# Hybrid diffusion step on one core: output DMAs moved from ScalarE to SyncE, two weight splits moved later, and one mask of the decays' rest moved from ScalarE to GpSimd

## The chip, the cores and the metric

The kernel runs on 1 core of one Trainium2 chip. The metric is the device time in microseconds of one execution. Three runs of the kernel before gave 833.46, 833.5 and 834.12 us, median 833.5.

## The reference, cut to what matters

Two trunk layers, each the same: a modulated RMSNorm, one input projection whose columns go to three head groups, one output projection, then a mixture of experts. The third head group is a Mamba-2 scan in chunks of 128 tokens, done in two directions. Its decays are what one part of the change touches:

```python
da = (dt * a)                        # per token, head and direction
cs = jnp.cumsum(da, axis=-1)
seg = cs[..., :, None] - cs[..., None, :]
lmat = jnp.exp(jnp.where(lower, seg, -jnp.inf))
scores = jnp.einsum('bclhn,bcshn->bhcls', cm, bm) * lmat
y_diag = jnp.einsum('bhcls,bcshp->bclhp', scores, xd)
chunk_states = jnp.einsum('bclhn,bhcl,bclhp->bchpn', bm, decay_to_end, xd)
...
o = jnp.concatenate([o_a, o_b, o_c], axis=-1)
return o @ w_out, new                # new: a_k, a_v, b_k, b_v, h_f, h_b of the context tokens
```

There are 384 tokens in 3 tiles of 128: tile 0 holds the context tokens, tiles 1 and 2 the latent ones. The six members of `new` are outputs of the kernel (keys and values of tile 0, and the two final states of tile 0).

## The kernel before, in words

Each engine has its own program. All of them walk the same list of steps, `layer_steps(l)`, and do of each step what concerns them. The order of that list is therefore the order on every engine. Engines meet in semaphores.

*Weights.* Weights come from memory as fp32 in pieces of 1 MB (128x2048) into `ring`, a ring of 8 slots of which the attention part uses 5. SyncE (SP) issues these loads one after the other, in the order of the list `pieces`; before each it waits until the former piece in that slot is released. A piece of `w_ada` is released by the TensorE (PE) matmuls that use it (L620), a piece of `w_out` by the subtraction of its split. `pieces` follows the step list, so moving a step `("wsplit", 0)` moves the load of that piece of `w_out` and shifts which slots later pieces take.

*Splits.* The big products take a weight as the sum of two parts: ScalarE (ACT) copies the piece to a rounded type (`w_hi`, L1225 for the input projection, L1216 for the output projection) and VectorE (DVE) subtracts this from the original (L1644 and L1639). A step `("w_split", p)` does this for piece p of the input projection, a step `("wsplit", n)` for unit n of the output projection. Piece 4 is first needed by `("rows", 4, 0)`, unit 0 of the output projection by `("wout",)` at the end of the attention.

*The stage around the scan.* `("rows", p, m)` is half a product of the input projection for token tile m (L854, 12 matmuls). ACT then copies the finished rows of tile m out of PSUM (L1385 and L1387). Between these products stand, for each tile m:
- `("ssm_in", m)`: PE transposes (L891, L895, L901). GpSimd (POOL) writes `ud[:, 0]`, the triangular mask times the rounded decays, for both directions (L2118, two instructions of 128x1024). POOL waits for the former tile's `seg`, and after the masks it makes `yx` and `xdd` (L2130, L2135). ACT copies `xs` (L1415) and writes `cbw` in 8 instructions (L1425). DVE makes `skip` (L1863) and multiplies `cbw` (L1871).
- `("seg", m)`: PE sums the masks (L924). It waits for POOL's half of `ud` (`sig["ud"]`) and for ACT's half (`sig["ud_lo"]`). ACT takes the exponential (L1433), then writes the half for the next tile, `masked_rest(m + 1)` (L1231): the mask times the decays' rest, in 16 instructions of 128x128, 8 for each direction. DVE multiplies to `mm` (L1881).
- `("ssm_y", m)`: PE products (L938, L948 or L954). DVE adds `yx` to them (L1888), and for tiles 1 and 2 makes `hin` (L1897, L1904). For tile 0, ACT copies the state to `stout` (L1441) and issues two output DMAs (L1445).
- `("prep", m)`: normalisation and rotation of the rows on DVE (L1830 to L1840, L1668 to L1676), with two small ACT instructions. For tile 0, ACT then waits for DVE's end of it and issues four output DMAs (L1398).

*PSUM banks.* Seven banks are given out in turn, in PE's order. Four of these hand-overs matter: the second half of `seg` of tile 1 takes the bank of the rows of tile 1 (freed by L1387). The rows of tile 2, second group, take the bank of `ssm_y` of tile 0 (freed by L1888). The first `rows` with p = 4 take the bank of the transposed queries (freed by L1406). The second half of `seg` of tile 2 and the rows of tile 1, third group, take banks that DVE frees in L1888 and L1904 of tile 1.

*The attention.* `head_steps()` gives 12 pairs of heads: `scores` v (PE L987, L993, L1001; DVE maximum L1928; ACT exponential L1465), `scale` v (DVE L1949 to L1955), `turn` v (PE L1011, ACT L1481), `values` (PE L1026, DVE L1963), and `gate` (DVE L1981). Pieces of `w_ada` (PE L620) are strewn between. The step `("wsplit", 0)` stands ahead of `("scores", 4)`. `ada_turn` (PE L633) needs ACT's copy of the `ada` bank (L1202).

*Order on the queues.* ACT does its two sets of output DMAs in order among its other work. SP has nothing to issue between the last load for the rows and the first `w_ada` piece behind them.

Of the kernel before, what the change touches and what calls it, by code (L numbers as in the profile page):

```python
# [25 lines left out]
P = 128  # L26
# [6 lines left out]
SH, SG, DS = 8, 2, 512  # L33
# [168 lines left out]
def layer_steps(l):  # L202


    ada = [("ada", l, t, k) for t in (1, 2) for k in range(KD)]
    ahead = [("ada", l + 1, 0, k) for k in range(KD)] if l + 1 < DEPTH else []
    early = 3 if l else 0
    s = [("norm", 0)] + ada[:early] + [("w_split", 0), ("h_split", 0), ("w_split", 1), ("h_split", 1), ("w_split", 2), ("xbc",)]
    s += [("rows", p, m) for p in (0, 1) for m in range(TILES)]

    def rows(g, m):
        return [("rows", 2 * g, m), ("rows", 2 * g + 1, m)]
    s += [("rest",), ("ssm_in", 0)] + rows(1, 0) + [("seg", 0), ("prep", 0), ("w_split", 4)] + rows(1, 1)
    s += [("ssm_y", 0), ("ssm_in", 1), ("seg", 1), ("prep", 1)] + rows(1, 2) + [("w_split", 5), ("turn_qk", 0)]
    s += [("ssm_y", 1), ("ssm_in", 2), ("rows", 4, 0), ("seg", 2), ("rows", 4, 1), ("rows", 4, 2), ("turn_qk", 1), ("prep", 2)]
    s += [("rows", 5, m) for m in range(TILES)] + [("ssm_y", 2), ("silu_z",)]
    burst = early + 3
    s += ada[early:burst]
    heads = head_steps()
    at = heads.index(("scores", 2))  # L220
    heads[at:at] = [("ssm_off", 1)]
    at = heads.index(("scores", 3))
    heads[at:at] = [("ssm_off", 2)]
    at = heads.index(("scores", 4))
    heads[at:at] = [("wsplit", 0)]
    at = heads.index(("scores", 2))
    heads[at:at] = [("turn_qk", 2)]
    rest = ada[burst:8] + [("ada_turn", l, 1)] + ada[8:14]
    done = 0
    for i, h in enumerate(heads):  # L230
        s.append(h)
        want = min(len(rest), len(rest) * (i + 1) * 3 // (len(heads) * 2)) if i < len(heads) // 3 else \
            len(rest) // 2 + (len(rest) - len(rest) // 2) * (i + 1 - len(heads) // 3) // (len(heads) - len(heads) // 3)
        s += rest[done:want]
        done = want
    s += [("turn_mix",)] + ada[14:] + [("ada_turn", l, 2), ("wsplit", 1), ("wout",), ("norm", 1)] + ahead[:3]
    s += [("router",), ("hrow", 0), ("rank",), ("hrow", 1), ("hrow", 2), ("h_lo",)] + ahead[3:] + [("flag",)]
    if ahead:
        s.append(("ada_turn", l + 1, 0))
    return s + [("combine",)] + moe_steps(0) + [("more",)]  # L240


def build(nc, a, a_out):
# [73 lines left out]
    with ExitStack() as ctx:  # L317
# [805 lines left out]
        @block.sync  # L1123
        def _(sp):
            sp.dma_start(pcol, a["pcol"]).then_inc(pcol_in, 16)
            for half in range(2):
                sp.dma_start(xT[:, 4 * half:4 * half + 4, :], a["xT"][:, 4 * half:4 * half + 4, :]).then_inc(x_in[half], 16)

            def load(key):
                dst = slot(key)  # L1130
                kind, l, at = key[0], key[1], key[2:]
                if kind == "first":
                    src = a["first"][at[0]]
                elif kind == "ada":
                    t, k = at
                    src = a["w_ada"][l, k * P:(k + 1) * P, t * PIECE:(t + 1) * PIECE]
                elif kind == "xbc":
                    src, dst = a["w_xbc"][l, at[0]], dst[:, 0:2 * (XBC + DT)]
                elif kind == "win":
                    src = a["w_rows"][l, at[0]]  # L1140
                elif kind == "wout":
                    src = a["w_out"][l, OUT_UNITS[at[0]][0], OUT_UNITS[at[0]][1]]
                elif kind == "down":
                    src = a["w_down"][l, at[1]].rearrange("(f p) n -> p f n", p=P)
                    dst = dst.rearrange("p (f n) -> p f n", f=2)
                else:
                    src = a["w_gu"][l, at[1], 0 if kind == "gua" else 1]
                sp.dma_start(dst, src).then_inc(landed(key)[0], 16)

            until_experts = pieces[0:pieces.index(("gua", 0, 0, 0))]  # L1150
            for n, key in enumerate(pieces):
                if n == 3:
                    sp.dma_start(const, a["const"]).then_inc(const_in, 16)
                if n == RING + KD // 2:
                    sp.dma_start(par, a["par"]).then_inc(par_in, 16)
                former = former_in[key]
                if made_here(key):
                    continue
                if former:
                    sp.wait_ge(*release[former])  # L1160
                if place[key] < HELD and key not in until_experts:
                    sp.wait_ge(*done["down", 0, 0, NE - 1])
                load(key)
                l = key[1]
                if key != ("down", l, 0, NE - 1):
                    continue

                sp.wait_ge(sig["flag"], l + 1)
                over = sp.value_load(flag[0:1, l:l + 1], min_val=0, max_val=1)
                with sp.If(over != 0):  # L1170
                    for former in pieces[n - (RING - HELD) + 1:n + 1]:
                        sp.wait_ge(*release[former])
                    for i, extra in enumerate(more_pieces):
                        extra = (extra[0], l, *extra[1:])
                        if i >= RING - HELD:
                            former = more_pieces[i - (RING - HELD)]
                            sp.wait_ge(*release[(former[0], l, *former[1:])])
                        load(extra)
                    sp.wait_ge(*done["down", l, PASSES - 1, NE - 1])
            for c in range(0, KD, 2):  # L1180
                sp.wait_ge(*modulated(DEPTH, 0, c + 1))
                sp.dma_start(a_out[0][:, c:c + 2, :], hT[:, c:c + 2, :]).then_inc(y_out, 16)
            sp.wait_ge(y_out, 16 * KD // 2)
            for s in out_sem:
                sp.wait_ge(s, 16 * DEPTH)
# [3 lines left out]
        def _(act):  # L1189
# [36 lines left out]

            def masked_rest(m):

                for d, tri in enumerate(("incl_f", "incl_b")):
                    for h in range(SH):  # L1230
                        ins = act.activation(ud[:, 1, d, h, :], c_(tri), ACT.Copy,  # L1231
                                             scale=da_lo[:, m, SH * d + h:SH * d + h + 1])
                ins.then_inc(sig["ud_lo"], 1)
# [91 lines left out]
            for l in range(DEPTH):  # L1325
                for step in STEPS[l]:
# [61 lines left out]
                    elif kind == "prep":  # L1388
# [2 lines left out]
                        act.activation(nrm[:, 8:14], nrm[:, 0:6], ACT.Ln, bias=eps_col, scale=1.0 / HD).then_inc(act_step, 1)  # L1391
                        act.wait_ge(act_step, act_steps())
                        act.activation(nrm[:, 16:22], nrm[:, 8:14], ACT.Exp, scale=-0.5).then_inc(sig["brs"], 1)
                        if m == 0:

                            act.wait_ge(sig["prep"], per["prep"] * l + 1)
                            for i, c0 in enumerate((256, 384, OFF_B + 256, OFF_B + 384)):
                                act.dma_start(a_out[1 + i][0, l].rearrange("s k d -> s (k d)"), row[:, 0, c0:c0 + P])\  # L1398
                                    .then_inc(out_sem[i], 16)
                    elif kind == "turn_qk":  # L1400
                        m = arg[0]
                        for t in range(2):
# [33 lines left out]
                    elif kind == "ssm_y":  # L1436
                        if arg[0] == 0:
                            key = ("state", l, 0)
                            act.wait_ge(*full(key))
                            src = bank(key)  # L1440
                            ins = act.copy(stout.rearrange("p a b n -> p (a b n)"), src)  # L1441
                            ins.then_inc(*was_read(key))
                            act.wait_ge(*taken(key))
                            for d in range(2):
                                act.dma_start(a_out[5 + d][0, l].rearrange("(r h) p n -> (h p) r n", h=2),  # L1445
                                              stout[:, d, :, :]).then_inc(out_sem[4 + d], 16)
                    elif kind == "silu_z":

                        for m in range(TILES):
# [654 lines left out]
        def _(pool):  # L2104
# [4 lines left out]
            for l in range(DEPTH):  # L2109
                for step in STEPS[l]:  # L2110
# [6 lines left out]
                    for d, tri in enumerate(("incl_f", "incl_b")):  # L2117
                        ins = tt(ud[:, 0, d, :, :], c_(tri).unsqueeze(1).to_broadcast((P, SH, P)),  # L2118
                                 da_hi[:, m, 8 * d:8 * d + 8].bitcast(F32).unsqueeze(2).to_broadcast((P, SH, P)), ALU.mult)
                    ins.then_inc(sig["ud"], 1)  # L2120
                    if m == 0:
                        pool.wait_ge(*taken(("cum", l)))
# [52 lines left out]
```

## Time and profile before

| | us |
|---|---|
| median of 3 runs | 833.5 |
| the profiled execution | 832.95 |
| its span in the profile | 831.2 |
| PE busy / share of the span | 764.6 / 92% |
| PE weight loads | 574.4 / 69% |
| DVE | 586.2 / 71% |
| ACT | 477.7 / 57% |
| POOL | 46.2 / 6% |
| mean granted TensorE clock | 0.975 |

1.75 us of the profiled execution lie around the span. A busy share is a mean over the whole span. The stage of the change lies at about 84 to 146 us and its attention at 146 to 203 us in the first layer; in the second layer the same steps lie 396.7 us later up to the first `seg` and about 395 us later after it. The experts' part follows, up to 412 and 808 us.

### The profile page before, as it was taken

How to read it: one execution, taken by the hardware profiler on the slowest of the kernel's cores; microseconds unless marked ns; L12 is line 12 of the kernel's file. 1: busy time of each engine (PE TensorE's matmuls, PEld its weight loads, DVE VectorE, ACT ScalarE, POOL GpSimd, SP SyncE). 2: the span in 40 equal slices, each digit the busy share in tenths (PEclk: the TensorE clock that was granted, in tenths of full speed). 3: DMA queues.
4: the chain of work that ended last, by engine and by line, in shares of the span. 5: the costliest groups of instructions: out<-in, count | busy, mean ns of one | idle time of the engine just before them, and what ended most of it. 6: DMA issues, size and time to landing. Idle time of an engine off the chain costs nothing.

```text
span 831.2 us, 10722 instructions
## 1 busy us (share of the span) xinstructions
PE 764.6 (92%) x3980; PEld 574.4 (69%) x3980; DVE 586.2 (71%) x934; ACT 477.7 (57%) x768; POOL 46.2 (6%) x36
## 2 busy tenths in 40 slices
PE   4997989789999999999989998988998799999995
PEld 2565868356956888888766786844694688888874
DVE  4139676776359889999663866678544888999975
ACT  3043983465336777777543387456533687777752
POOL 0000631000000000000000063100000000000000
PEclk9999999979999999999999999989998999999998
DMA  9942032976437799999760213377540079999912
GB/s 366 423 172 100 3 126 58 415 285 255 153 151 278 262 377 358 373 374 359 266 277 19 61 42 110 119 304 255 209 146 0 22 251 377 365 366 377 355 63 79
DMA packets 33488, 185.98 MB, mean 224 GB/s; under 512 B 5136, under 2 KB 6288, under 8 KB 16400
## 3 DMA queue, kind: packets, MB, share of 16 engines
q1 hardware_dynamic: 30160, 184.11, 58.5%
q10 hardware_dynamic: 3264, 1.05, 0.5%
q8 instruction: 36, 0.59, 0.3%
q14 instruction: 28, 0.23, 0.1%
HBM read 182.53 MB, written 2.62 MB: 223 GB/s over the span
## 4 chain that ended last, share of the span: by engine, by line
PE 64%; DVE 7%; ACT 6%; issue 2%; ACTq 0%; DVEq 0%
PE psum L739 21%; PE psum L768 11%; PE psum L1056 8%; PE psum L854 4%; PE psum L825 4%; PE psum L791 3%; PE psum L620 2%; ACT ud L1231 2%; PE psum L1026 2%; PE psum L1070 1%; DVE h_lo L2064 1%; PE psum L1011 1%; PE psum L987 1%; PE psum L717 1%; PE psum L752 1%
## 5 line engine op out<-in xcount | busy, mean ns | idle before, releaser
L1724 DVE TENSOR_TENSOR split<-ring,split 128x2048 fp32r<-128x2048 f32 x96 | 219.9, 2291 | 27.7 <-ACT split L1306 25.1
L1306 ACT CAST split<-ring 128x2048 fp32r<-128x2048 f32 x96 | 183.6, 1912 | 18.2 <-PE psum L768 14.5
L739 PE MATMUL psum<-split,y_hi 128*128 128x512 f32 x512 | 162.8, 399 | 0.0
L739 PEld LDWEIGHTS psum<-split,y_hi 128*128 128x128 f32 x512 | 93.7, 188 | 19.6
L739 PE MATMUL psum<-split,y_lo 128*128 128x512 f32 x256 | 100.6, 393 | 0.0
L854 PE MATMUL psum<-ring_r,hT_hi 128*128 128x512 f32 x216 | 75.2, 403 | 6.2 <-ACT qkT L1406 3.6
L768 PE MATMUL psum<-split,hidT 128*128 128x512 f32 x256 | 70.3, 396 | 1.8 <-DVE hidT_lo L1729 1.8
L825 PE MATMUL psum<-hT,ring 128*128 128x384 f32 x192 | 69.2, 499 | 0.0
L768 PEld LDWEIGHTS psum<-split,hidT 128*128 128x128 f32 x256 | 47.4, 187 | 14.5 <-DVE hidT_lo L1729 3.7
L739 PEld LDWEIGHTS psum<-split,y_lo 128*128 128x128 f32 x256 | 48.0, 188 | 11.1
L854 PEld LDWEIGHTS psum<-ring_r,hT_hi 128*128 128x128 f32 x216 | 41.0, 193 | 16.6 <-issue 4.4
L2118 POOL TENSOR_TENSOR ud<-const,da_hi 128x1024 fp32r<-128x1024 f32 x12 | 27.2, 2288 | 437.8 <-DVE da_lo L1821 437.4
L825 PEld LDWEIGHTS psum<-hT,ring 128*128 128x128 f32 x192 | 34.2, 190 | 20.2 <-issue 2.5
L1246 ACT ACTIVATE row<-xT 128x384 f32<-128x384 f32 x40 | 20.4, 524 | 48.1 <-DVE xT L1656 44.8
L620 PE MATMUL psum<-ring,silu_c 128*32 128x512 f32 x320 | 41.2, 620 | 3.7 <-DMA ring<-in_w_ada 3.2
L1465 ACT ACTIVATE hT<-psum,att 128x384 f32<-128x384 f32 (+1 forms) x48 | 24.0, 506 | 35.6 <-DVE att L1936 19.0
L1656 DVE SCALAR_TENSOR_TENSOR xT<-psum,mods,xT 128x128 f32<-128x128 f32 x64 | 23.6, 413 | 25.0 <-PE psum L1056 20.5
L768 PE MATMUL psum<-split,hidT_lo 128*128 128x512 f32 x128 | 39.8, 392 | 0.0
L854 PE MATMUL psum<-w_hi,hT_hi 128*128 128x512 f32 x72 | 29.6, 412 | 4.3 <-DVE dtw L1775 4.3
L1056 PE MATMUL psum<-m_hi,split 128*128 128x384 f32 x128 | 33.4, 337 | 0.0
L1056 PE MATMUL psum<-o_hi,split 128*128 128x384 f32 x128 | 33.2, 336 | 0.0
L1639 DVE TENSOR_TENSOR split<-ring,split 128x2048 fp32r<-128x2048 f32 x8 | 18.3, 2292 | 17.7 <-ACT split L1216 17.7
(258 smaller groups left out, 1340.4 us busy)
## 6 DMA issues: line engine op xcount, KB each, us to landing
ring<-in_w_gu SPq DMA_DIRECT2D x64, 1024.0 KB, 5.0
ring<-in_w_ada SPq DMA_DIRECT2D x40, 1024.0 KB, 6.3
ring<-in_w_down SPq DMA_DIRECT2D x32, 1024.0 KB, 5.3
ring<-in_w_rows SPq DMA_DIRECT2D x12, 1024.0 KB, 4.9
ring<-in_first SPq DMA_DIRECT2D x8, 1024.0 KB, 14.7
ring<-in_w_out SPq DMA_DIRECT2D x8, 1024.0 KB, 5.0
ring<-in_w_xbc SPq DMA_DIRECT2D x8, 784.0 KB, 8.5
par<-in_par SPq DMA_DIRECT2D x1, 1632.0 KB, 12.1
```

The source lines that it names most:

```text
L620: last = pe.matmul(psum[32 * q:32 * q + 32, 7, :], silu_c[:, k, :], w[:, q * 512:(q + 1) * 512], start=(k == 0), stop=(k == KD - 1), skip_ ...
L739: last = pe.matmul(dst, x[:, g, t, :], w[:, j, :], start=(t == 0 and i == 0), stop=(t == KD - 1 and i == 2))
L768: last = pe.matmul(psum[:, b, :], x, w[:, half * 512:(half + 1) * 512], start=(e % EPG == 0 and i == 0), stop=(e % EPG == EPG - 1 and i == ...
L791: last = pe.matmul(dst[:, 0:TOK], src[:, g, c * P:(c + 1) * P], selT[:, g, :], start=(i == 0 and g == 0), stop=(i == 1 and g == NG - 1))
L825: last = pe.matmul(bank(("xbc", l, c))[:, 0:TOK], w[:, kk, c * P:(c + 1) * P], hT[:, k, :], start=(k == 0), stop=(k == KD - 1))
L854: last = pe.matmul(dst, x[:, k, tok], w[:, j, :], start=(k == 0 and i == 0), stop=(k == KD - 1 and i == 2))
L1056: last = pe.matmul(dst[:, 0:TOK], w[:, k, cols], x[:, k, :], start=(part == 1 and k == 0 and i == 0), stop=(part == 0 and k == 3 and i == 2))
L1306: act.copy(splits[n % SPLITS][:, 0, :], slot(key)).then_inc(raised("whi", l, p), 1)
L1465: act.activation(probs[:, u % 8, 0:w], src[:, 0:w], ACT.Exp, bias=att[:, 1, u:u + 1], scale=SCALE, accum_out=att[:, 2, u:u + 1]).then_inc( ...
L1656: ins = stt(xT[:, c, part], src[:, part], mods[:, l, gate + c, j:j + 1], xT[:, c, part], ALU.mult, ALU.add)
L1724: tt(lo, slot(unit_key(l, p, n)), hi.bitcast(F32), ALU.subtract).then_inc(raised("wlo", l, p), 1)
L2118: ins = tt(ud[:, 0, d, :, :], c_(tri).unsqueeze(1).to_broadcast((P, SH, P)), da_hi[:, m, 8 * d:8 * d + 8].bitcast(F32).unsqueeze(2).to_bro ...
```

## The change

- The four row outputs and the two state outputs of each layer are issued by SP, in a new function `store(l)`, just before the first `w_ada` load behind the pieces of the rows. ACT loses the wait for `prep` and six DMA issues in each layer.
- `("w_split", 4)` moves from behind `("prep", 0)` to behind `("ssm_in", 1)`, ahead of `("seg", 1)`.
- `("wsplit", 0)` moves from ahead of `("scores", 4)` to behind `("scale", 11)`, the last of the scales.
- `masked_rest(m)` for m = 1 and 2 does only the second direction on ACT (8 instructions in place of 16). POOL does the first direction in one instruction of 128x1024 more, behind its two of the same tile.

```diff
-    s += [("rest",), ("ssm_in", 0)] + rows(1, 0) + [("seg", 0), ("prep", 0), ("w_split", 4)] + rows(1, 1)
-    s += [("ssm_y", 0), ("ssm_in", 1), ("seg", 1), ("prep", 1)] + rows(1, 2) + [("w_split", 5), ("turn_qk", 0)]
+    s += [("rest",), ("ssm_in", 0)] + rows(1, 0) + [("seg", 0), ("prep", 0)] + rows(1, 1)
+    s += [("ssm_y", 0), ("ssm_in", 1), ("w_split", 4), ("seg", 1), ("prep", 1)] + rows(1, 2) + [("w_split", 5), ("turn_qk", 0)]
...
-    at = heads.index(("scores", 4))
+    at = heads.index(("scale", PAIRS - 1)) + 1
     heads[at:at] = [("wsplit", 0)]
...
+            def store(l):
+                sp.wait_ge(sig["prep"], per["prep"] * l + 1)
+                for i, c0 in enumerate((256, 384, OFF_B + 256, OFF_B + 384)):
+                    sp.dma_start(a_out[1 + i][0, l].rearrange("s k d -> s (k d)"), row[:, 0, c0:c0 + P]).then_inc(out_sem[i], 16)
+                sp.wait_ge(*taken(("state", l, 0)))
+                for d in range(2):
+                    sp.dma_start(a_out[5 + d][0, l].rearrange("(r h) p n -> (h p) r n", h=2), stout[:, d, :, :])\
+                        .then_inc(out_sem[4 + d], 16)
+            behind_rows = [pieces[pieces.index(("w_hi", l, 5)) + 1] for l in range(DEPTH)]
...
+                if key in behind_rows:
+                    store(key[1])
...
-                for d, tri in enumerate(("incl_f", "incl_b")):
+                for d, tri in ((0, "incl_f"), (1, "incl_b"))[1 if m else 0:]:
...
-                        if m == 0:
-                            act.wait_ge(sig["prep"], per["prep"] * l + 1)
-                            for i, c0 in enumerate((256, 384, OFF_B + 256, OFF_B + 384)):
-                                act.dma_start(...)
...
-                            act.wait_ge(*taken(key))
-                            for d in range(2):
-                                act.dma_start(...)
...
+                    if m:
+                        ins = tt(ud[:, 1, 0, :, :], c_("incl_f").unsqueeze(1).to_broadcast((P, SH, P)),
+                                 da_lo[:, m, 0:8].unsqueeze(2).to_broadcast((P, SH, P)), ALU.mult)
                     ins.then_inc(sig["ud"], 1)
```

## Rows read from the trace of the kernel before

**Rows 1.** Chain of waits, second layer: start us, us, engine, tile, line.
```profile
494.79 4.74 ACT ud L1231 x16
...
503.09 1.90 ACT ring_r L1225
...
507.61 3.20 ACT cbw L1425 x8
...
511.76 4.73 ACT ud L1231 x16
...
556.52 1.81 ACT split L1216
...
558.42 2.29 DVE split L1639
560.72 0.94 DVE att L1928 x2
```

**Rows 2.** Timeline, PE weight loads; in brackets idle time before and its releaser.
```profile
505.59 0.76 PEld L924 LDWEIGHTS psum<-ud,sides 128*128 128x128 f32 x4 [1.11 <-ACT row L1387]
508.04 0.19 PEld L854 LDWEIGHTS psum<-ring_r,hT_hi 128*128 128x128 f32 x1 [1.69 <-DVE ring_r L1644]
519.75 0.19 PEld L854 LDWEIGHTS psum<-ring_r,hT_hi 128*128 128x128 f32 x1 [1.95 <-issue]
524.76 0.19 PEld L854 LDWEIGHTS psum<-ring_r,hT_hi 128*128 128x128 f32 x1 [0.51 <-issue]
...
129.13 0.19 PEld L854 LDWEIGHTS psum<-ring_r,hT_hi 128*128 128x128 f32 x1
...
162.47 0.13 PEld L620 LDWEIGHTS psum<-ring,silu_c 128*32 128x32 f32 x4 [2.63 <-DMA ring<-in_w_ada]
...
168.44 0.18 PEld L633 LDWEIGHTS psum<-const,ada_rows 128*128 128x128 f32 x1 [4.78 <-ACT ada_rows L1202]
```

**Rows 3.** Timeline, POOL, second layer: the masks of tiles 1 and 2.
```profile
493.94 3.76 POOL L2118 TENSOR_TENSOR ud<-const,da_hi 128x1024 fp32r<-128x1024 f32 x2 [0.22 <-PE psum L924]
...
512.10 4.07 POOL L2118 TENSOR_TENSOR ud<-const,da_hi 128x1024 fp32r<-128x1024 f32 x2
```

**Rows 4.** Timeline, DVE: second layer's scan stage, then the first layer's attention.
```profile
495.92 2.19 DVE L1830 TENSOR_TENSOR tmp<-row 128x384 f32<-128x384 f32 x1
...
512.21 1.29 DVE L1881 TENSOR_TENSOR mm<-psum,cbw 128x512 f32<-128x512 f32 x2
...
524.22 0.42 DVE L1904 TENSOR_TENSOR hin<-psum,hin 128x256 f32<-128x256 f32 x1
...
159.99 0.48 DVE L1955 TENSOR_SCALAR hT<-hT,att 128x128 f32<-128x128 f32 x2
162.88 2.29 DVE L1639 TENSOR_TENSOR split<-ring,split 128x2048 fp32r<-128x2048 f32 x1 [2.40 <-ACT split L1216]
...
171.47 1.02 DVE L1928 TENSOR_REDUCE att<-psum 128x1 f32<-128x384 f32 x2 [1.68 <-PE psum L1001]
```

**Rows 5.** Timeline, ACT's queue, second layer: the output issues.
```profile
501.18 1.81 ACTq L1398 DMA_DIRECT2D out<-row  x4
...
506.06 0.95 ACTq L1445 DMA_DIRECT2D out<-stout  x2
```

**Rows 6.** Timeline, PE, first layer: the scores of pair 6.
```profile
172.88 1.22 PE L987 MATMUL psum<-qkT 64*128 64x256 f32 x4
```

**Rows 7.** Timeline, SP's queue, first layer: the load of output unit 0.
```profile
148.95 0.33 SPq L1148 DMA_DIRECT2D ring<-in_w_out  x1
```

**Rows 8.** Stretches: us, busy of PE, PEld, DVE, ACT, POOL; granted clock, DMA share, GB/s.
```profile
123.00:127.00 4.00, 3.90 (x10) 3.11 (x11) 3.97 (x6) 3.88 (x10) 0.00 (x0) 0.57 0.20 82
...
160.00:168.40 8.40, 1.45 (x11) 0.35 (x10) 5.89 (x11) 4.72 (x15) 0.00 (x0) 0.76 1.01 422
168.40:175.40 7.00, 6.93 (x36) 4.00 (x36) 4.10 (x13) 1.92 (x9) 0.00 (x0) 0.56 0.64 268
...
553.00:566.00 13.00, 10.10 (x54) 5.43 (x57) 10.14 (x26) 4.92 (x15) 0.00 (x0) 0.65 0.54 212
```

More of the change, by code:

```diff
@@ L1393, in _ @@
                         act.activation(nrm[:, 16:22], nrm[:, 8:14], ACT.Exp, scale=-0.5).then_inc(sig["brs"], 1)
-                        if m == 0:
-                            act.wait_ge(sig["prep"], per["prep"] * l + 1)
-                            for i, c0 in enumerate((256, 384, OFF_B + 256, OFF_B + 384)):
-                                act.dma_start(a_out[1 + i][0, l].rearrange("s k d -> s (k d)"), row[:, 0, c0:c0 + P])\
-                                    .then_inc(out_sem[i], 16)
                     elif kind == "turn_qk":
@@ L1440, in _ @@
                             src = bank(key)
-                            ins = act.copy(stout.rearrange("p a b n -> p (a b n)"), src)
-                            ins.then_inc(*was_read(key))
-                            act.wait_ge(*taken(key))
-                            for d in range(2):
-                                act.dma_start(a_out[5 + d][0, l].rearrange("(r h) p n -> (h p) r n", h=2),
-                                              stout[:, d, :, :]).then_inc(out_sem[4 + d], 16)
+                            act.copy(stout.rearrange("p a b n -> p (a b n)"), src).then_inc(*was_read(key))
                     elif kind == "silu_z":
```

## The prediction, written before the result was known

> **What bounds the kernel now.** I read the page's chain of waits first. In the experts' part it is PE from end to end, and nothing there is touched. In the second layer's scan stage and attention it leaves PE for ACT and DVE, and those are the steps that the change moves [rows 1]. The chain of the first layer is only followed from 167 us on, so there I read PE's idle time in the timeline. It shows the same stalls of PE 396.7 us earlier.
>
> In the scan stage PE stops four times in the second layer [rows 2]. At 505.59 it waits 1.11 us for the row copy that frees a bank. At 508.04 it waits 1.69 us for DVE, which stands in the split of piece 4. At 519.75 it waits 1.95 us for the copy of the transposed queries. At 524.76 it waits 0.51 us for the bank that DVE's L1904 frees, started at 524.22 [rows 4]. The first two are waits for ACT's issues and for split 4, which the chain holds at 503.09 [rows 1].
>
> In the attention of the first layer PE stands still for most of 160 to 168.4 us: 1.45 us busy in 8.4 [rows 8]. First it waits 2.63 us for a `w_ada` piece, then 4.78 us for ACT's `ada` copy [rows 2]. ACT is late because DVE's maximum of pair 4 is queued behind output split 0: DVE waits 2.40 us for ACT's half and then works 2.29 us [rows 4]. The second layer has the same in its chain: 1.81 us of ACT's half, 2.29 us of DVE's, then the maximum at 560.72 [rows 1].
>
> **Part 1: scan stage.** Second layer, by its own clock times.
>
> ACT loses half of the masks of tiles 1 and 2. Sixteen took 4.74 and 4.73 us [rows 1], so 2.37 us each time. It loses the issues, 1.81 + 0.95 us [rows 5], the wait for `prep` in front of them, and split 4 (1.90 us, [rows 1]) up to a later place. The issues cost SP the same 2.8 us, and there they are hidden: SP issues nothing until the rows of tile 2 are done, and both waits of `store` end before that. I put this part at 0.
>
> ACT would so reach `cbw` of tile 1 some 8 us sooner, but PE's product of tile 0 has to be ready first, and that stays where it is, at about 503. I let `cbw` start at 503.85 in place of 507.61 [rows 1], 3.8 us sooner. So the two stalls of 1.11 and 1.69 go, and PE does the rows of tile 2 from 505.3 in place of 508.04.
>
> What is late next is DVE. In front of its `mm` of tile 1, at 512.21 before [rows 4], now stands split 4: `cbw` done 507.0, ACT's half 1.90 to 508.9, DVE's half 2.29 more. Beside it POOL does three masks in place of two. One takes 3.76/2 = 1.88 us [rows 3]. DVE's L1830, issued at 495.92 beside POOL's pair, took 2.19 us and ended at 498.11, 0.41 us after the pair at 497.70 [rows 3, 4]. So a DVE instruction with two SBUF inputs waits for the end of the POOL instruction that runs. That makes up to 1.88 us for each POOL instruction met, and I count 0.75 for split 4: `mm` then starts at 508.9 + 0.75 + 2.25 = 511.9. PE arrives for it at 511.5 and waits 1.6 us for its end at 513.1, where it came at 514.2 before.
>
> The Trainium skill has this as a rule (SBUF — State Buffer, "Who interferes with whom"): the pair shared by DVE and GpSimd is an exclusive lock for a whole instruction. The trace agrees, by the 2.19 us.
>
> From `mm` to L1904 DVE is busy without a gap, 524.22 − 512.21 = 12.0 us [rows 4]. With the same sequence behind 511.9 and one more lock of 0.1 to 1.9 us (I take 0.1: the maximum of two instructions that wait already) L1904 comes at 524.0, 0.25 us sooner. PE's next products wait for it, so the stage gives **0.25 us in the second layer**, although ACT gave up 9 us. Bounds: 2.7 us sooner if nothing on DVE is late, and 3.5 us later if DVE's half of the split and one instruction behind it each meet one full POOL mask more.
>
> In the first layer the same point is at 129.13, not at 524.76 − 396.7 = 128.06 [rows 2]. PE was the later one there, since its clock was at its lower level (granted 0.57) from 123 to 127 [rows 8]. If DVE sets the time now in this layer too, PE gets there at 127.8: **1.3 us in the first layer**, low clock or not. Bounds: 3.5 later and 3.7 sooner, as above.
>
> **Part 2: attention, first layer.** DVE ends the scale of pair 2 at 160.47 [rows 4], in the new timing 1.3 sooner, at 159.1. With no split ahead of it the maximum of pair 4 starts there, in place of 162.88 + 2.2 = 165.1: 6.0 us sooner. ACT's exponential and `ada` copy follow, if the last piece of `w_ada` is there. The load of output unit 0 stood before it on SP [rows 7], at 422 GB/s [rows 8] 1.05 MB = 2.48 us of a saturated DMA. It goes to the back, so the piece lands 1.3 + 2.48 = 3.8 us sooner, at 158.7 in place of 162.47, just behind PE's scores 4. So the wait of 2.63 goes nearly whole, and `ada_turn` comes at 162.4 in place of 168.44 [rows 2]. In the new list `scores 5` stands ahead of it, so PE fills the gap of the copy.
>
> What comes last from here: DVE does the maximum 4, scale 3 and the gate until 162.8, and maximum 5 there in place of 171.47 [rows 4]: 8.7 us sooner. PE does `scores 6` at 164.0 in place of 172.88 [rows 6]: 8.9 us. Part of this is clock: from 168.4 to 175.4 PE ran at a granted 0.56 after its 8.4 us of idleness [rows 8], and I count about 1.6 us of that as saved, since the stops left are of 1.2 us at most. From there on PE is busy almost without a gap to the end, with all pieces landed ahead, so 8.9 us carry through.
>
> At the end split 0 stands behind the last scale. ACT's half (1.9) delays the copies of the last two `turn`s. PE's fifth block of `values` works from pairs 8 and 9 meanwhile and covers most of it. I take 1.0 us as left, of 0 to 1.9. DVE's half is before `turn_mix`, where DVE idles. Sum of the first layer: −8.9 + 1.0 = **−7.9 us**, the 1.3 of its stage included.
>
> **Attention, second layer.** DVE's maximum of pair 4 could start 4.6 us sooner, at 556.05 (scale 2 and `mods` end then) in place of 560.7 [rows 1]. But PE ran at a granted 0.65 over 553 to 566 [rows 8], and its `scores 5` ended at 560.5, so that the next maximum is only 3.6 us sooner. At `turn` 4 and `scores` 7 I still find 2.7 to 2.8. The clock may recover sooner, as PE loses its stops of 560 to 564: then up to 4.6. I take **−3.0**, with 0.25 of the stage in it. At the end PE comes to `values` 5 as the copies are done: 0.
>
> **Sum.** −7.9 − 3.0 = −10.9 on the profiled execution's own time, 832.95 (span 831.2 and 1.75 around it): 822.1. The median of the runs stands 0.55 above that execution, so the forecast is 822.6.
>
> **Rivals.**
>
> *A. Only one of the two stalls of the first layer is collected.* The DMA has a share of 1.01 over 160 to 168.4 [rows 8], so the queue may stay full and the piece come late, or the low clock return in the gap that is left. For it: both stalls lie behind each other. Against it: the load that goes away is as long as the wait. Then the first layer gives its stage's 1.3, the 2.48 of the load and 0.5 more, −4.3, and the second −2: 833.5 − 6.3 = 827.2.
>
> *B. The mask gives nothing or costs.* The Trainium skill warns (Perfetto Trace Analysis, "Optimizing Scalar/DVE Operations") that moving work between GpSimd and DVE may not help, because they share a port. That is this rival in general form. By rows: two further masks of 1.88 us in each layer [rows 3] held against DVE's chain of 12.0 us, −0.25 and −1.3 become +1.6 and +0.6, the rest unchanged: 822.6 + 3.8 = 826.4.
>
> *C. Slower: DVE loses the port in the scan stage.* Split 4 waits for one whole mask more before `mm`, and the first and the fifth instruction of `prep` 1 for one each: 3 × 1.88 = 5.6 us a layer [rows 3]. PE, which waits for `mm` and for L1904, then stands long enough for its clock to fall as it did at 123 us, where 4 us at 0.57 cost 4 × 0.43 = 1.7 us [rows 8]. The stages so give +7.3 in each layer in place of −0.25 and −1.3, beside the attention's −9.35: 833.5 + 14.6 − 9.35 = 838.8. It decides from 9.35 / 2 = 4.7 us a layer. For it: DVE's later instructions there mostly have two SBUF inputs, and the clock did fall in this stage. Against it: POOL's pair with one DVE instruction let in between took 4.07 in place of 3.76 us [rows 3], so the two take turns, and `mm` itself reads PSUM.
>
> *D. No change*, as PE's later work only waits elsewhere: the experts' part has PE in the chain throughout, and begins when the output projection ends, so I see no place.
>
> **How the numbers follow.** Forecast 0.55, A 0.17, B 0.17, C 0.07, D 0.04. The range reaches from 818.5 (the second layer gives 4.6, the stages 1 us each more, the tail nothing) up to A with a fall of the clock on top, 829.5. A measurement of this kernel tells 0.2% (1.7 us) from no change. Faster 0.55 + 0.17 + 0.17 = 0.89, same 0.04, slower 0.07.
>
> **What would show it.** ACT's `cbw` of tile 1 3 to 4 us sooner, but DVE's L1904 by under 1 us. The load of output unit 0 behind thirteen `w_ada` loads of the layer, and not behind seven. PE's stop before `ada_turn` in the first layer about 1.2 us in place of 4.78, and the granted clock near 1.0 behind it. Output projection from about 194.9 in place of 202.8. If L1904 comes over 2 us later than before in its layer, B or C is true; if PE still waits over 2 us for the `w_ada` piece, A is. The forecast is wrong if the interval from first `scores` to output projection shrinks by less than 5 us in the first layer.

## The result: 12 us faster, 821.4 us for a forecast of 822.6

The changed kernel takes 821.36 us (median of 4 runs, 819.86 to 825.34), the kernel before 833.48 beside it (4 runs, 832.57 to 834.12). The ratio is 0.9863, 95% interval 0.9826 to 0.9900. The profiled execution took 819.86, its span is 817.7 us in place of 831.2, and its mean granted clock (TensorE's clock as the hardware granted it, 1.00 being the upper of its two levels) 0.989 in place of 0.975.

The span is 13.5 us shorter. Read at fixed points of PE's program (milestones) in both traces, these are: 0.2 before the first layer's stage, 1.2 in its scan stage up to the product behind L1904, 0.1 from there to the scores of pair 0, 6.2 in its attention. Then 0.3 in the experts' part, 0.1 in the second layer's scan stage, 4.7 in its attention, and 0.6 behind it. So the two attentions give 11 of 13.5 us; the scan stages, from which ACT lost most work, 1.3.

PE's stops that answer to [rows 2], from the timeline of the weight loads (idle time before and its releaser in brackets). L1644, L1881, L1888, L1904 of before are L1646, L1883, L1890, L1906 here.

```profile
505.31 1.86 PEld L938 LDWEIGHTS psum<-xs,mm 128*128 128x128 f32 x16 [1.65 <-DVE mm L1883]
510.20 0.30 PEld L854 LDWEIGHTS psum<-ring_r,hT_hi 128*128 128x128 f32 x2 [1.38 <-issue]
515.27 0.77 PEld L924 LDWEIGHTS psum<-ud,sides 128*128 128x128 f32 x4 [1.56 <-DVE y L1890]
516.55 0.30 PEld L854 LDWEIGHTS psum<-ring_r,hT_hi 128*128 128x128 f32 x2 [0.52 <-issue]
...
127.69 0.30 PEld L854 LDWEIGHTS psum<-ring_r,hT_hi 128*128 128x128 f32 x2 [0.51 <-issue]
...
158.46 0.16 PEld L620 LDWEIGHTS psum<-ring,silu_c 128*32 128x32 f32 x8 [0.16 <-DMA ring<-in_w_ada]
162.18 0.42 PEld L633 LDWEIGHTS psum<-const,ada_rows 128*128 128x128 f32 x4 [1.39 <-ACT ada_rows L1215]
187.72 0.66 PEld L1026 LDWEIGHTS psum<-pT,row 128*64 128x64 f32 x8 [1.13 <-issue]
```

The stops of 1.11 and 1.69 us are gone and others stand there: 1.65 for DVE's `mm`, 1.56 for its L1890. In the attention the 2.63 us for the `w_ada` piece are 0.16, the 4.78 for ACT's copy 1.39. PE's scores of pair 6, at 172.88 before [rows 6]:

```profile
163.56 0.70 PE L987 MATMUL psum<-qkT 64*128 64x256 f32 x4
```

DVE in the second layer's scan stage, which answers to [rows 4]. DVE is busy without a gap from the half split at 500.74 to L1906 at 516.01:

```profile
498.94 1.28 DVE L1873 TENSOR_TENSOR cbw<-cbw,psum 128x512 f32<-128x512 f32 x2 [2.12 <-ACT cbw L1432]
500.74 3.30 DVE L1646 TENSOR_TENSOR ring_r<-ring,ring_r 128x2048 fp32r<-128x2048 f32 x1 [0.52 <-ACT ring_r L1238]
503.97 1.28 DVE L1883 TENSOR_TENSOR mm<-psum,cbw 128x512 f32<-128x512 f32 x2
505.17 1.05 DVE L1832 TENSOR_TENSOR tmp<-row 128x384 f32<-128x384 f32 x1
506.72 1.67 DVE L1670 TENSOR_TENSOR tmp<-row,const 128x384 f32<-128x384 f32 x1
...
516.01 0.42 DVE L1906 TENSOR_TENSOR hin<-psum,hin 128x256 f32<-128x256 f32 x1
```

POOL beside it [rows 3], with the new mask (L2123), and ACT's `cbw` with the split behind it [rows 1]:

```profile
485.83 3.76 POOL L2120 TENSOR_TENSOR ud<-const,da_hi 128x1024 fp32r<-128x1024 f32 x2 [0.23 <-PE psum L924]
489.54 2.21 POOL L2123 TENSOR_TENSOR ud<-const,da_lo 128x1024 fp32r<-128x1024 f32 x1
...
500.00 5.80 POOL L2120 TENSOR_TENSOR ud<-const,da_hi 128x1024 fp32r<-128x1024 f32 x2
505.76 2.21 POOL L2123 TENSOR_TENSOR ud<-const,da_lo 128x1024 fp32r<-128x1024 f32 x1
```

```profile
495.71 3.20 ACT cbw L1432 x8
498.91 1.81 ACT ring_r L1238
```

SP's queue, first layer: the stores, and the load of output unit 0 at its new place (148.95 before, [rows 7]).

```profile
103.94 1.78 SPq L1154 DMA_DIRECT2D out<-row  x4
106.50 0.94 SPq L1157 DMA_DIRECT2D out<-stout  x2
...
165.54 0.33 SPq L1148 DMA_DIRECT2D ring<-in_w_out  x1
```

The stretches of [rows 8] (us; busy of PE, PEld, DVE, ACT, POOL; granted clock; DMA share; GB/s). The clock stood at 0.57, 0.76 and 0.65 in them and is at its upper level (1.00) in all three. The second layer lies some 8 us earlier here; over the same steps of it, 544.8 to 557.8, the clock is 1.00 too.

```profile
123.00:127.00 4.00, 2.88 (x13) 2.02 (x13) 3.99 (x5) 2.75 (x7) 0.00 (x0) 1.00 0.00 0
160.00:168.40 8.40, 6.59 (x56) 4.27 (x56) 8.05 (x25) 5.59 (x21) 0.00 (x0) 1.00 1.01 420
553.00:566.00 13.00, 11.33 (x92) 6.30 (x92) 11.76 (x37) 11.16 (x40) 0.00 (x0) 1.00 0.50 173
```

This holds for this execution only. The same kernel was profiled once more later (e9 below); there the clock fell in both scan stages and in the second attention:

```profile
123.00:127.00 4.00, 4.00 (x14) 3.11 (x14) 3.97 (x7) 2.88 (x8) 0.00 (x0) 0.71 0.00 0
511.50:515.50 4.00, 4.00 (x13) 3.11 (x12) 3.95 (x6) 2.42 (x7) 0.00 (x0) 0.63 0.01 2
545.00:558.00 13.00, 11.19 (x72) 6.31 (x71) 11.09 (x34) 6.76 (x27) 0.00 (x0) 0.77 0.52 181
```

### The profile page after: what moved, and what is told of

Read it like the earlier page. It is cut to its first block, busy times and chain, and to the rows that moved or that the text cites. A ratio compares the mean times of both kernels' runs of the same rounds, so it can differ in the third digit from the quotient of the medians.

```text
span 817.7 us, 10694 instructions
## 1 busy us (share of the span) xinstructions
PE 756.0 (92%) x3980; PEld 570.2 (70%) x3980; DVE 589.0 (72%) x934; ACT 468.1 (57%) x736; POOL 58.4 (7%) x40
## 4 chain that ended last, share of the span: by engine, by line
PE 76%; DVE 14%; ACT 5%; issue 4%; DMA 1%; DVEq 0%; ACTq 0%; SPq 0%
PE psum L739 22%; PE psum L768 11%; PE psum L854 10%; PE psum L1056 8%; PE psum L825 7%; PE psum L791 3%; PE psum L620 2%; PE psum L1070 1%; DVE att L1930 1%; DVE h_lo L2066 1%; PE psum L817 1%; DVE ring_r L1646 1%; PE psum L717 1%; PE psum L661 1%; PE psum L752 1%
## 5 line engine op out<-in xcount | busy, mean ns | idle before, releaser
L1726 DVE TENSOR_TENSOR split<-ring,split 128x2048 fp32r<-128x2048 f32 x96 | 219.9, 2290 | 27.6 <-ACT split L1319 25.0
L739 PEld LDWEIGHTS psum<-split,y_hi 128*128 128x128 f32 x512 | 93.7, 188 | 19.6
L2120 POOL TENSOR_TENSOR ud<-const,da_hi 128x1024 fp32r<-128x1024 f32 x12 | 30.7, 2577 | 430.0 <-DVE da_lo L1823 429.5
L1325 ACT CAST hidT<-psum 128x256 fp32r<-128x256 f32 x32 | 11.9, 373 | 31.3 <-PE psum L752 31.3
```

The costliest lines, as they stand in the source:

```text
L739: last = pe.matmul(dst, x[:, g, t, :], w[:, j, :], start=(t == 0 and i == 0), stop=(t == KD - 1 and i == 2))
L1726: tt(lo, slot(unit_key(l, p, n)), hi.bitcast(F32), ALU.subtract).then_inc(raised("wlo", l, p), 1)
```

## The experiments

Every kernel's profile was read at the same points. Times in us from PE's first transposes of tile 0 (`ssm_in` 0, L891) of the layer, first / second layer: *rows* is PE's product behind L1906 (L1904 before), *scores* the scores of pair 0, *w_out* the output projection's first product.

| kernel | rows | scores | w_out | median (range), runs |
|---|---|---|---|---|
| before | 42.06 / 40.97 | 61.74 / 60.50 | 115.47 / 112.12 | 833.48 (832.57–834.12), 4 |
| after | 40.86 / 40.86 | 60.42 / 60.38 | 107.91 / 107.34 | 821.36 (819.86–825.34), 4 |
| e1 before, out split late | 41.98 / 41.86 | 61.67 / 61.50 | 109.14 / 109.08 | 823.97 (822.71–825.29), 4 |
| e2 after, out split early | 40.88 / 40.87 | 60.44 / 60.38 | 113.81 / 111.99 | 831.34 (830.43–832.98), 10 |
| e3 after, no third mask | 39.76 / 39.76 | 59.32 / 59.32 | 106.81 / 106.85 | 819.93 (817.46–821.96), 4 |
| e4 after, split 4 ahead of `ssm_y` 0 | 39.62 / 39.46 | 60.01 / 60.25 | 107.48 / 107.92 | 821.24 (819.80–823.20), 4 |
| e5 e4, no third mask | 38.21 / 38.23 | 57.77 / 57.77 | 105.24 / 105.39 | 819.38 (814.39–820.84), 4 |
| e6 after, outputs on ACT | 43.23 / 43.21 | 62.88 / 62.85 | 110.35 / 109.77 | 823.59 (823.14–826.82), 4 |
| e7 split 4 at old place, no third mask | 37.67 / 37.69 | 57.23 / 57.21 | 104.71 / 104.14 | 813.45 (812.53–815.51), 4 |
| e8 e7 with the third mask | 38.73 / 38.73 | 59.52 / 59.87 | 106.99 / 107.53 | 820.19 (816.83–822.03), 4 |

Beside e1 to e4 the kernel before took 833.78 (831.83 to 835.60, 13 runs), beside e5 to e8 834.54 (832.33 to 835.21, 7 runs). My theory was the forecast's: attention by the out split alone, scan stage held by DVE. The rival: ACT's release in the scan stage is what the attention's gain rests on, and the mask is worth its cost.

**e1, only the out split late.** In the kernel before:

```diff
-    at = heads.index(("scores", 4))
+    at = heads.index(("scale", PAIRS - 1)) + 1
```

> The kernel before with only the step wsplit 0 moved behind the last scale. Theory (the two gains are separate): the attention gives what it gave in the changed kernel, about 6.4 us in the first layer (its 7.8 less the 1.4 of the scan stage) and 4.6 in the second, so 833.5 - 11.0 = 822.5; PE's stop before ada_turn in the first layer is about 1.4 us, and the granted clock is 1.0 in both attentions. Rival (the scan stage's order is what lets the attention keep its clock): the first layer gives 6 us, the second only the 2.75 that the waits alone are worth, with a granted clock near 0.65 behind its first scores: 825.

Measured: ratio 0.9888 (0.9862 to 0.9914). From scores to w_out 47.5 and 47.6 us in place of 53.7 and 51.6: 6.3 and 4.0 saved with the old scan stage. The median lies between the 822.5 of the theory and the rival's 825. The second attention gave 4.0 where 4.6 was expected, and its clock was not at 1.00 but at a granted 0.88 over 547.2 to 560.2. That is not the rival's doing: the changed kernel's own second execution (e9) takes 47.56 us there, as e1 does. PE's stop before `ada_turn` is 1.47 us, as expected.

The second layer's scan stage came out 0.9 us longer than in the kernel before's own profile. The trace shows the low clock that the kernel before had only in its first layer, at the same steps:

```profile
513.00:517.00 4.00, 4.00 (x11) 3.19 (x12) 3.95 (x6) 3.73 (x10) 0.00 (x0) 0.60 0.16 66
```

With it, the old scan stage takes 41.9 to 42.1 us up to the rows, without it 41.0.

**e2, everything but the out split.** The reverse of that edit, in the changed kernel.

> The changed kernel with wsplit 0 back ahead of scores 4: all parts of the scan stage and none of the attention. Theory: the time from the first ssm_in to the rows of tile 1, third group, shrinks by 1.2 to 1.4 us in the first layer (the low clock goes) and by 0.1 to 0.25 in the second, and the stops of 2.6 and 4.8 us at w_ada and ada_turn stay: 832. Rival (ACT's 9 us a layer were the bound of the stage): over 4 us in each layer, 825.

Measured: ratio 0.9975 (0.9963 to 0.9987). The stage's 1.2 and 0.1 us are there, and PE's stops in the attention too: 2.64 us, and 3.80 where 4.8 was expected. The two halves add up in the medians: 9.8 + 2.4 = 12.2 us, and the whole gave 12.1. The rival falls.

**e3, the third mask back on ACT.**

```diff
-                for d, tri in ((0, "incl_f"), (1, "incl_b"))[1 if m else 0:]:
+                for d, tri in ((0, "incl_f"), (1, "incl_b")):
...
-                    if m:
-                        ins = tt(ud[:, 1, 0, :, :], ...)
```

> The changed kernel with the sixteen masks of tiles 1 and 2 back on ACT and no third mask on GpSimd. Theory (the stage is bound by DVE, and each GpSimd mask holds DVE's two-input instructions): the tile-1 instruction L1670, 1.67 us beside the third mask, takes 0.56, so DVE's L1906 comes 1.1 us sooner in each layer, 2.2 us faster than the changed kernel, 819.2. Rival (ACT's time counts): ACT's 2.4 us for each tile go back on the path, 3 to 5 us slower than the changed kernel, 825.

Measured: ratio 0.9832 (0.9800 to 0.9864). The rows come 1.10 us sooner in each layer, with eight more instructions on ACT. DVE's two instructions behind `mm`, in e3's timeline:

```profile
506.41 1.05 DVE L1832 TENSOR_TENSOR tmp<-row 128x384 f32<-128x384 f32 x1
...
507.96 0.55 DVE L1670 TENSOR_TENSOR tmp<-row,const 128x384 f32<-128x384 f32 x1
```

L1670 takes 0.55 in place of 1.67: it had waited for the mask at 505.76. That is the whole 1.1 us. The time expected was 819.2. The medians are only 1.4 us apart and their ranges overlap; the profile is the firmer witness here.

**e4 and e5, split 4 between its two places.** The two splits of the step list in e4 (e5 also drops the third mask, as in e3):

```diff
-    s += [("ssm_y", 0), ("ssm_in", 1), ("w_split", 4), ("seg", 1), ("prep", 1)] + ...
+    s += [("w_split", 4), ("ssm_y", 0), ("ssm_in", 1), ("seg", 1), ("prep", 1)] + ...
```

> The changed kernel with w_split 4 one step earlier, ahead of ssm_y 0, where ACT waits for PE. Theory (DVE's split in front of mm of tile 1 is what ate the stage's gain): ACT's half is done before the state is there, DVE's before GpSimd's masks start; mm comes at about 24 us behind the first ssm_in in place of 28.3, the stop of 1.65 us before L938 and that of 1.54 us before the second half of seg 2 go, and the rows of tile 1, third group, start 3.5 to 4 us sooner in each layer: 821.4 - 7.5 = 814. Rival (the masks' port is the bound, wherever the split stands): under 1 us a layer, 820.

> As e4 (w_split 4 ahead of ssm_y 0), and without the third GpSimd mask (ACT does sixteen again). In e4 DVE's mm came 3.65 us sooner than in the changed kernel but L1906 only 1.4, since two instructions of prep 1 waited for masks (1.58 in place of 1.0, 2.31 in place of 0.62). Theory (the masks' hold on DVE ate the rest): from mm to L1906 11 us as in e3, so the rows of tile 1, third group, start 36.5 to 37.2 us behind the first ssm_in of the layer, 2.6 to 3.3 sooner than e3's 39.76; e3's 819.9 less 5.5: 814.4. Rival (ACT's masks, back on its path, are now the bound): over 38.5, and 818 to 820.

e4 missed: ratio 0.9847 (0.9817 to 0.9877), 821.24 us where 814 was expected. The rows came 1.2 and 1.4 us sooner, not 3.5 to 4, so the rival (the masks' port) is nearer. Its DVE, second layer:

```profile
503.49 1.29 DVE L1883 TENSOR_TENSOR mm<-psum,cbw 128x512 f32<-128x512 f32 x2
504.70 1.58 DVE L1832 TENSOR_TENSOR tmp<-row 128x384 f32<-128x384 f32 x1
...
506.78 1.67 DVE L1670 TENSOR_TENSOR tmp<-row,const 128x384 f32<-128x384 f32 x1
508.37 2.31 DVE L1674 TENSOR_TENSOR tmp<-row,const 128x192 f32<-128x192 f32 x2
...
517.78 0.43 DVE L1906 TENSOR_TENSOR hin<-psum,hin 128x256 f32<-128x256 f32 x1
```

`mm` stands at 24.63 us of its layer in place of 28.28, but from it to L1906 are 14.3 us in place of 12.0: all three masks now fall behind `mm`, and three instructions of `prep` wait for one each. Then PE loses 3.05 us in one stop before the second half of `seg` of tile 2, and its clock falls:

```profile
517.00:536.00 19.00, 18.96 (x88) 15.72 (x90) 10.56 (x27) 4.73 (x9) 3.05 (x3) 0.91 0.34 119
```

Rows to scores take 20.4 and 20.8 us there; 19.6 in the changed kernel. e5, without the mask, is 1.5 us sooner at the rows than e3 and keeps the clock there: ratio 0.9806 (0.9767 to 0.9844).

e5 missed too. Its rows stand at 38.2 where 36.5 to 37.2 was expected, since from `mm` to L1906 are 13.1 us and not 11: the first two masks still make L1832 (2.05 us) and L1670 (1.67) wait. Its median, 819.38, is 5 us above the 814.4 expected. In its profile 3.3 us of this lie ahead of the first layer's stage (it starts at 90.85, e3's at 87.55), in code that is the same in both.

**e6, the outputs back on ACT.** `store(l)` is taken out of SP's list, and the wait for `prep` and the six `dma_start` stand in ACT's again, as before.

> The changed kernel with the six output DMAs of each layer back on ACT. Theory: ACT's issues (1.8 and 0.95 us and the wait for prep) stand between PE's first product and cbw of tile 1; cbw, split 4 and mm come about 1.5 to 2 us later, and so do DVE's L1906 and the rows behind it: 42.4 to 42.9 us behind the first ssm_in in place of 40.86, 821.4 + 3.5 = 824.9. Rival (ACT has slack now that its masks and split 4 are gone from there): under 0.3 us a layer, 821.5.

Measured: ratio 0.9874 (0.9856 to 0.9892), 2.4 us later at the rows in both layers. ACT and PE in its timeline, second layer:

```profile
497.14 1.80 ACTq L1409 DMA_DIRECT2D out<-row  x4
498.99 0.37 ACT L1396 COPY row<-psum 128x256 f32<-128x256 f32 x1 [3.48 <-issue]
...
500.15 0.95 ACTq L1455 DMA_DIRECT2D out<-stout  x2
501.22 0.58 ACT L1426 COPY xs<-psum 128x512 f32<-128x512 f32 x1 [1.10 <-issue]
...
512.06 3.31 PEld L938 LDWEIGHTS psum<-xs,mm 128*128 128x128 f32 x16 [4.05 <-DVE mm L1891]
```

The issues hold the two small copies, then `xs`, `cbw`, the split and with it `mm`. PE stands 4.05 us, and the weight loads behind take 3.31 in place of 1.86: the clock fell (granted 0.53 over 512 to 517). `cbw` starts 1.65 us later in its layer than in the changed kernel and `mm` 2.4. The other 0.75 us is the half split's, which takes 4.06 us here in place of 3.30, waiting longer for GpSimd's pair. DVE's half split stands in front of `mm` in both kernels; the issues only make it later. The rows came 0.3 us later than the 42.4 to 42.9 expected, and the rival falls. The Trainium skill (DMA: Bandwidth & Descriptors, "Issuing engines are not separate DMA queues") says that issuing from several engines saves only sequencer time, usually small beside the DMA; here that time was 2.75 us of the engine ahead of the critical product, and 2.4 us of the layer.

**e7 and e8, split 4 at its old place.** e7: outputs on SP and the late out split alone, split 4 where the kernel before has it, no third mask. e8 is e7 with the third mask.

```diff
-    s += [..., ("seg", 0), ("prep", 0)] + rows(1, 1)
-    s += [("ssm_y", 0), ("ssm_in", 1), ("w_split", 4), ("seg", 1), ("prep", 1)] + ...
+    s += [..., ("seg", 0), ("prep", 0), ("w_split", 4)] + rows(1, 1)
+    s += [("ssm_y", 0), ("ssm_in", 1), ("seg", 1), ("prep", 1)] + ...
```

> The changed kernel with w_split 4 back in its old place (behind prep 0) and without the third GpSimd mask: what is left is the outputs on SP and the late output split. Theory (the outputs on ACT were all that made the old place costly): split 4 runs on DVE in 2.3 us in which it waits for PE, nothing of DVE is late, the rows of tile 1, third group, come at 36.5 to 37.2 as in e5, 814.4. Rival (the old place delays the row copies that seg 1's bank waits for, or the first product's bank): one more stop of PE of 0.5 to 1.2 us ahead of the rows of tile 2, 816 to 817.

> The changed kernel with w_split 4 back in its old place, the third GpSimd mask kept. Theory (mask price is the same wherever the split stands once DVE is the bound): 2 to 2.5 us a layer later at the rows of tile 1, third group, than e7, as e4 against e5; about 819.5. Rival (the mask pays by freeing ACT): equal to or below e7.

e7 is the fastest: ratio 0.9759 (0.9735 to 0.9783), its rows 3.2 us before the changed kernel's in both layers. The time is as expected, the rows 0.5 us later. e8: 0.9822 (0.9792 to 0.9852), its rows 1.05 us behind e7's, where 2 to 2.5 was expected.

e7 and e1 differ in one thing only: who issues the outputs. From e1 to e7 the rows come 4.3 and 4.2 us sooner, and 3.3 us sooner than in the kernel before's second layer, whose clock had not fallen. So the outputs on SP alone give more in the scan stage than the whole change does. The changed kernel, e7 and e8 were measured again side by side (e9, e10 and e11), since e7 and e8 lay 6.7 us apart in the medians and 8.6 in the profiled executions, of which 3.0 lay ahead of the first layer's stage, in code that is the same in both. Granted clock (the number before the last two) over 70 to 80 us, e7, then e8:

```profile
70.00:80.00 10.00, 10.00 (x39) 8.03 (x38) 9.72 (x23) 2.63 (x5) 0.00 (x0) 0.86 0.01 2
```

```profile
70.00:80.00 10.00, 8.82 (x27) 7.01 (x28) 9.65 (x27) 1.57 (x3) 0.00 (x0) 0.66 0.10 41
```

> The changed kernel once more, beside the next two on one chip, to tell the worth of the mask and of the split's place from the luck of the clock: the stretch of 60 to 95 us, which no kernel here changes, ran some 3.5 us longer in some profiles, at a lower granted clock in 70 to 80 us. Both theories expect 821 +- 2 and rows of tile 1 at 40.86 us behind the layer's first input projection step in both layers.

> The changed kernel with split 4 at its old place and without the third GpSimd mask, again. If the order of the engines sets the time: 813 to 815, about 7 below the changed kernel. If the first measurement was luck of the clock: within 4 of the changed kernel, 817 to 818.

> The same with the third GpSimd mask kept. By the stages of its first profile (1.05 us at the rows and 1.2 to 1.6 behind them, per layer) the mask costs 4.5 to 5.5 us in all: 818 to 819. If the difference to the version without it (6.7 us in the medians before) was half luck of the clock, 2 us for the rows alone: 815 to 816.

Measured, beside the kernel before at 833.16 (831.22 to 835.74, 9 runs): changed kernel 819.72 (819.37 to 822.83), 0.9850 (0.9826 to 0.9875); e7 814.99 (812.50 to 815.39), 0.9767 (0.9745 to 0.9789); e8 817.93 (816.49 to 821.53), 0.9819 (0.9792 to 0.9846); 5 runs each. So e7 is 5 us faster than the changed kernel by the medians (6.5 by the means), where about 7 was expected. The third mask costs 3 (4 by the means), less than the 4.5 to 5.5 expected. The intervals within the layer repeat: e8's rows at 38.72 and 38.73, e7's at 37.70 and 37.69. The changed kernel's are at 40.90 and 41.01, where 40.86 was expected, with the clock low at 123 and 511.5 as shown above; its second attention takes 47.56 us in place of 46.96. DVE behind `mm` in the second layer, e7, then e8:

```profile
498.28 1.29 DVE L1883 TENSOR_TENSOR mm<-psum,cbw 128x512 f32<-128x512 f32 x2
499.49 1.51 DVE L1832 TENSOR_TENSOR tmp<-row 128x384 f32<-128x384 f32 x1
...
501.50 1.67 DVE L1670 TENSOR_TENSOR tmp<-row,const 128x384 f32<-128x384 f32 x1
503.09 0.61 DVE L1674 TENSOR_TENSOR tmp<-row,const 128x192 f32<-128x192 f32 x2
```

```profile
499.22 1.29 DVE L1883 TENSOR_TENSOR mm<-psum,cbw 128x512 f32<-128x512 f32 x2
500.43 0.84 DVE L1832 TENSOR_TENSOR tmp<-row 128x384 f32<-128x384 f32 x1
...
501.78 1.67 DVE L1670 TENSOR_TENSOR tmp<-row,const 128x384 f32<-128x384 f32 x1
503.37 2.31 DVE L1674 TENSOR_TENSOR tmp<-row,const 128x192 f32<-128x192 f32 x2
```

The pair alone already costs e7 two waits (L1832, L1670); the third mask adds the one before L1674, 1.70 us, less 0.67 at L1832. PE's stop before the second half of `seg` of tile 2 and the stretch behind it, e7, then e8:

```profile
510.06 0.76 PEld L924 LDWEIGHTS psum<-ud,sides 128*128 128x128 f32 x4 [0.73 <-DVE y L1890]
...
511.00:528.00 17.00, 16.89 (x88) 13.93 (x86) 9.85 (x25) 4.95 (x10) 3.05 (x3) 1.00 0.40 136
```

```profile
512.04 0.77 PEld L924 LDWEIGHTS psum<-ud,sides 128*128 128x128 f32 x4 [2.32 <-DVE y L1890]
...
512.00:532.00 20.00, 19.85 (x94) 15.89 (x98) 11.27 (x28) 5.43 (x10) 3.04 (x3) 0.91 0.36 126
```

After a stop of 0.73 us the clock stays up, after 2.32 it fell here and cost 1.5 us more (rows to scores 21.1 in place of 19.55). In the first layer of this same execution the clock stayed up after the same stop; in e8's first profile it cost 1.2 and 1.6. So the fall is likely after such a stop, not certain.

## Why the prediction was right, point by point

- *ACT's `cbw` 3.8 us sooner, `mm` of tile 1 at 511.9, PE waiting 1.6 us for it.* `cbw` came 3.8 us sooner within the layer. The second layer's stage lies 8.1 us earlier, so 511.9 means 503.8: measured 503.97, wait 1.65. Two small errors partly cancelled: split 4 met more lock than taken (3.30 − 2.29 = 1.01 us, not 0.75), and ACT's half took 1.81 us, not 1.90.
- *Scan stage 0.25 and 1.3.* Measured 0.11 and 1.20. The prediction said "low clock or not", and e9 bears this out: with the clock at 0.71 and 0.63 there, the rows come only 0.04 and 0.15 us later than with it at 1.00. That the two layers' gains differ lies in the kernel before, whose profiled execution had the low clock in one layer only. Against e1, which had it in both, the stages give 1.1 and 1.0 us.
- *Mask at 1.88 us, costing almost nothing.* The size was wrong, 2.21 us, and the cost too: 1.1 us per layer (e3). In the sum it stayed unseen, since the lock on L1670 is there before and after (1.67 us in both traces). Before, the pair beside `mm` caused it; after, the pair had moved away and the new mask took its place. That DVE's 12.0 us would stay was true, by replacement and so by luck. Rival B was right on the mechanism; it priced 1.85 to 1.9 us a layer, and 1.1 was measured at the rows.
- *Store on SP at 0.* Right: both sets were issued by 107.4 us, the next load at 114.4. What its removal from ACT was worth was never priced alone; e6 gives 2.4 us per layer.
- *Attention, first layer, 6.6 without its stage, tail included.* Measured 6.2. `ada_turn` at 162.4 forecast, 162.18 measured; scores 6 at 164.0, 163.56; stop before values 5 1.0, 1.13.
- *Attention, second layer, 2.75 without its stage.* The mis-sized term: 4.65 measured, 4.06 in e9's execution of the same kernel and 4.04 in e1. The forecast's own upper end was 4.6, since "the clock may recover sooner", and over the same steps the granted clock went from 0.65 to 1.00 (0.77 in e9, 0.88 in e1). I should have put the clock's return into the middle here, as I had in the first layer, where the same stops go.
- *Rivals.* A needed over 2 us of wait for the piece: 0.16 was left. C needed 4.7 us per layer of port loss in the scan stage: the change as a whole lost none. D is out by the result.
- *The range.* Its two ends do not come out of the terms given: these give 818.0 and 828.9 (827.2 and one fall of the clock, 1.7), not 818.5 and 829.5. Nor does one measurement tell 1.7 us: the interval came out 3 us to either side. Neither changes the outcome.

Missed in the working: it treated the outputs, split 4's new place and the mask as one part with one answer. Apart, at the rows of each layer, starting from the changed kernel: outputs on SP give 2.4; the mask costs 1.1; with the mask gone, split 4 behind `ssm_in` 1 costs 2.1 (39.76 against 37.67) over its old place, and the time in front of `mm` is then DVE's half split. Read from the kernel before, with split 4 at its old place, the outputs give 3.3 us, or 4.2 to 4.3 against e1. So two parts of the change gave back what the third had won. The forecast of the time was right with a stage in which gains and losses cancelled, and it did not see that most of the stage's gain was to be had by leaving two parts out. The 0.6 us behind the second attention is no gain of the change: from the output projection to the end of the span are 235.3 us before, 234.7 after and 233.8 in e9, the same kernel. What stays open: why the clock falls in one execution and not in the next.

## What to carry to other kernels

When several edits of one stage relieve the same engine, price them singly against the engine that is next: here ACT gave up 9 us and the stage moved by 0.1 to 1.2, because the half split had come to stand ahead of the product that PE waits for. One of the edits alone moved it by 3.3 to 4.3. Before GpSimd takes over a 128x1024 product in fp32, list which DVE instructions with two SBUF inputs fall beside it; each can wait for the rest of that instruction. And value a stop of PE by what the clock does behind it: the second attention gave 1.3 to 1.9 us more than the 2.75 counted from the waits. Before a gain of 1 us is put down to an edit, profile the same kernel twice: one execution had the low clock in a stage and the next had not.

## What the runs showed of the hardware that was not expected

- A GpSimd product of the same shape (128x1024) took 1.88 us with the rounded decays and 2.21 us with the rest (L2120 and L2123); the two differ in the second input's data and tile. Why was not tried.
- POOL loses too: its pair took 5.80 us, in place of 3.76, where DVE's half split of 2.29 us ran beside it, and that split 3.30. In e6 the split took 4.06.
- Of DVE's instructions, `mm` (one input from PSUM) took 1.27 to 1.29 us beside masks and away from them, the reduction L1834 0.55; those with both inputs in SBUF took up to 1.7 us more than alone. This agrees with the Trainium skill (SBUF — State Buffer, "Who interferes with whom"), the exclusive lock for a whole instruction.
- The clock differs between executions in code that no edit touches: over 70 to 80 us 0.86 in e7's profile and 0.66 in e8's, and the first layer's scan stage then starts some 3 us later (90.4 in place of 87.4). e8's own kernel, profiled again, had 0.86 there. The four runs of the changed kernel spread over 5.5 us, as much as the mask and the split together are worth. Differences of 1 to 3 us were read from milestones within the layer for that reason.
